# Recurrent scan of layer 2: subtractions and products of the queries' side moved from GpSimd to VectorE

## The reference, cut to what matters

```
def hgrn2_scan(q, k, v, logf, s0):
    ...
    def step(S, inp):
        qc, kc, vc, gc = inp
        bcs = jnp.cumsum(gc, axis=1)
        o_inter = jnp.einsum('bthk,bhkv->bthv', qc * jnp.exp(bcs), S)
        diff = bcs[:, :, None] - bcs[:, None]
        dec = jnp.exp(jnp.where(mask[None, :, :, None, None], diff, -jnp.inf))
        att = jnp.einsum('bthk,btshk,bshk->bhts', qc, dec, kc)
        o_intra = jnp.einsum('bhts,bshv->bthv', att, vc)
        last = bcs[:, -1]
        S_new = S * jnp.exp(last)[..., None] + jnp.einsum(
            'bshk,bshv->bhkv', kc * jnp.exp(last[:, None] - bcs), vc)
        return S_new, o_inter + o_intra
```

## Time and profile before

| what | value |
|---|---|
| median of three runs | 2851.33 us |
| the profiled execution | 2844.31 us |
| its span | 2842.5 us |
| TensorE busy over the span | 2559.0 us (90%) |
| VectorE busy | 1454.2 us (51%) |
| ScalarE busy | 753.1 us (26%) |
| GpSimd busy | 803.5 us (28%) |

### The profile page before, as it was taken

The page is one execution under the profiler, slowest core; times in us unless marked ns, Lnnn a source line. Parts: engine busy times, 40 slices in busy tenths (PEclk is TensorE's granted clock), DMA queues, the critical chain, the costliest instruction groups (busy, mean ns, idle before and its releaser), DMA issues.

```text
span 2842.5 us, 30129 instructions
## 1 busy us (share of the span) xinstructions
PE 2559.0 (90%) x11915; PEld 1877.4 (66%) x11915; DVE 1454.2 (51%) x1956; ACT 753.1 (26%) x1265; POOL 803.5 (28%) x429
## 2 busy tenths in 40 slices
PE   5789999998988879999988967789999799989997
PEld 3789854446877778644468957685445699864444
DVE  6866643335746677433456489773333426640013
ACT  1223221003554442200033344421010333130111
POOL 3547300003543432000026479710000347500000
PEclk6899899998999998999989988879999899979999
DMA  7734659990321146499915410155989133538880
GB/s 267 246 108 122 206 188 348 344 347 31 109 87 60 60 126 215 168 338 343 354 39 170 133 36 22 33 178 214 348 326 338 60 105 104 152 123 300 298 297 36
DMA packets 291851, 524.41 MB, mean 184 GB/s; under 512 B 9472, under 2 KB 141056, under 8 KB 291328
## 3 DMA queue, kind: packets, MB, share of 16 engines
q1 hardware_dynamic: 288256, 519.33, 51.9%
q10 hardware_dynamic: 3456, 3.15, 0.3%
HBM read 517.73 MB, written 4.72 MB: 184 GB/s over the span
## 4 chain that ended last, share of the span: by engine, by line
PE 70%; DVE 12%; ACT 4%; issue 3%; DMA 2%; POOL 2%; ACTq 0%; SPq 0%; DVEq 0%
PE ps L1924 23%; PE ps L1941 12%; PE ps L1661 6%; PE ps L1662 5%; PE ps L1663 5%; PE ps L1729 2%; DVE uw L1352 2%; PE ps L1862 1%; PE ps L1886 1%; DVE macc L2017 1%; PE ps L1887 1%; POOL wlo L1591 1%; PE ps L1763 1%; PE ps L1962 1%; PE ps L1963 1%
## 5 line engine op out<-in xcount | busy, mean ns | idle before, releaser
L1591 POOL TENSOR_TENSOR wlo<-ring,whi 128x1024 fp32r<-128x1024 f32 x202 | 535.2, 2666 | 1428.6 <-ACT whi L1458 1428.6
L1924 PE MATMUL ps<-ring,xg 128*128 128x512 f32 x1536 | 702.8, 595 | 0.0
L1924 PEld LDWEIGHTS ps<-ring,xg 128*128 128x128 f32 x1536 | 280.9, 191 | 296.3 <-issue 296.0
L2017 DVE SCALAR_TENSOR_TENSOR macc<-ring,cond_s,macc 128x1024 f32<-128x1024 f32 x280 | 387.1, 1441 | 4.8 <-DMA ring<-w_mod 4.8
L2241 DVE SCALAR_TENSOR_TENSOR hid<-ps,cws,sg 128x256 f32<-128x256 f32 x96 | 46.4, 484 | 652.6 <-ACT sg L1552 652.6
L1941 PE MATMUL ps<-ring,hidt 128*128 128x512 f32 x768 | 351.2, 601 | 2.3 <-ACT hidt L1527 2.3
L1661 PE MATMUL ps<-hh,whi 128*128 128x384 f32 x840 | 302.8, 360 | 33.3 <-POOL wlo L1591 20.6
L1662 PE MATMUL ps<-hl,whi 128*128 128x384 f32 x840 | 290.8, 346 | 0.0
L1663 PE MATMUL ps<-hh,wlo 128*128 128x384 f32 x840 | 290.4, 346 | 0.0
L1458 ACT ACTIVATE whi<-ring 128x1024 fp32r<-128x1024 f32 x202 | 207.0, 1054 | 278.2 <-DMA ring<-gmlp_w_out 82.7
L1941 PEld LDWEIGHTS ps<-ring,hidt 128*128 128x128 f32 x768 | 147.1, 193 | 183.4 <-issue 183.4
(11 more groups left out here) (366 smaller groups left out, 4193.4 us busy)
## 6 DMA issues: line engine op xcount, KB each, us to landing
ring<-moe_w_gu SPq DMA_DIRECT2D x192, 1024.0 KB, 8.0
ring<-w_mod SPq DMA_DIRECT2D x96, 1024.0 KB, 8.3
ring<-moe_w_down SPq DMA_DIRECT2D x96, 1024.0 KB, 6.2
ring<-gmlp_w_in SPq DMA_DIRECT2D x32, 1024.0 KB, 6.3
ring<-ssd_w_in SPq DMA_DIRECT2D x21, 1024.0 KB, 5.3
ring<-hgrn_w_in SPq DMA_DIRECT2D x20, 1024.0 KB, 5.2
ring<-gmlp_w_out SPq DMA_DIRECT2D x16, 1024.0 KB, 6.8
ring<-ssd_w_out SPq DMA_DIRECT2D x8, 1024.0 KB, 5.9
```

Of the source, the lines that this page charges most:

```text
L1591: pool.tensor_tensor(split_sub(wlo, s0), raw_sub(s0), split_sub(whi, s0).bitcast(F32), ALU.subtract).then_inc(S["lo_ready"], 1)
L1924: ins = pe.matmul(ps[:, s % 2, :], xg[:, w, k, :], whole(what, s, 4)[:, k % 4, :], start=(k == 0), stop=(k == KD - 1))
L2017: ins = dve.scalar_tensor_tensor(out=acc[:, v, :], in0=w[:, k, :], scalar=by, in1=acc[:, v, :], op0=ALU.mult, op1=ALU.add)
```

## The change

The subtraction and the product of the queries' side move from GpSimd's program into VectorE's, each right behind its counterpart of the keys' side. Their operands and their arithmetic stay the same, as do the semaphores that they raise (`w_sub`, `wq_ready`). GpSimd keeps `hqe` and the weight splits.

```diff
@@ pool_hgrn
-            def decay(n):
-
-                h, j = n // LEVELS, LEVELS - 1 - n % LEVELS
-                if n >= 3:
-                    pool.wait_ge(S["lv_done"], step_of(n - 3) + 1)
-                out = uw_slot(n)[:, 1, :].rearrange("p (b two x) -> p b two x", two=2, x=1 << j)
-                pool.tensor_tensor(out, crossed(h, j), border(h, j, True), ALU.subtract).then_inc(S["w_sub"], 1)
-
-            decay(0)
             for n in range(LEVELS * HH):
                 h, j = divmod(n, LEVELS)
-                if n + 1 < LEVELS * HH:
-                    decay(n + 1)
-                pool.wait_ge(S["u_exp"], n + 1)
-                W = uw_slot(n)[:, 1, :]
-                pool.tensor_tensor(W, W, hq[:, h, :], ALU.mult).then_inc(S["wq_ready"], 1)
                 if j == 5:
                     pool.wait_ge(S["qe_exp"], h + 1)
...
@@ dve_hgrn, produce(g)
                 dve.tensor_tensor(out, border(h, j), paired(hf_flat, h, j), ALU.subtract).then_inc(S["u_sub"], 1)
+                out = uw_slot(g)[:, 1, :].rearrange("p (b two x) -> p b two x", two=2, x=1 << j)
+                dve.tensor_tensor(out, crossed(h, j), border(h, j, True), ALU.subtract).then_inc(S["w_sub"], 1)
@@ dve_hgrn, complete(g)
                 dve.tensor_tensor(out, out, paired(hk_flat, h, j), ALU.mult).then_inc(S["uw_ready"], 1)
+                W = uw_slot(g)[:, 1, :]
+                dve.tensor_tensor(W, W, hq[:, h, :], ALU.mult).then_inc(S["wq_ready"], 1)
```

## The result

The changed kernel took 2853.52 us, the median of 20 runs (2847.01 to 2859.52), against 2850.4 us for 20 runs of the kernel before on the same chip (2845.11 to 2852.87). The ratio is 1.0016, with an interval of 1.0009 to 1.0023: the means lie 4.5 us apart, the medians 3.1. So it is slightly slower. That lies inside the forecast range and within the 0.2% that I had called "same", but on the other side of zero: I had forecast 3 us faster. That the range holds it is owed to its width and not to the sum, of which two terms were off.

A forecast was written before the change was run, and what follows sets the result against it. VectorE was taken to bound the scan's levels. Its work -4.0, waits +1.5 and -0.5 ahead of the stretch summed to -3.0 us, from 2851.3 to 2848.3 us, called "same"; range 2837 to 2861.

The forecast's parts named there:

- What bounds the kernel: In the scan's levels, VectorE sets the length: busy 167.2 of 177.6 us, idle 10.4.
- The mechanism of the hold: VectorE operations with two SBUF operands stand still until GpSimd's ends: 1.0 us per `hqe`, 2.1 per split, 20.6 in all.
- The work of VectorE: In the levels, 52.1 us new work plus 20.6 remaining holding less 76.7 holding before: -4.0 us.
- Sum 142.5 us: VectorE's own operations in the levels after the change, without holding, priced from start to start in quiet places.
- The waits: VectorE's idle time in the levels would go from 10.4 to 11.9 us: +1.5 us.
- The new wait at the head's start: VectorE waits for ScalarE's exponent of level 3, 0.7 us in each of seven heads: 4.9 us.
- 4.0 ... two waits at the ends of heads 3 and 5 ... I keep these: VectorE's waits for the diagonal's products, 1.19 and 2.78 us, would stay as they were.
- a rival with a chance of 0.21: TensorE falls to its lower clock behind splits; 2.78 us in all six heads gives +10 us, 2861; chance 0.21.
- "-0.5 us" ahead of the stretch: Before the levels, VectorE's second decayed key, 0.82 us under GpSimd's first two subtractions, gets shorter: -0.5 us.
- Edits at nothing: ScalarE's exponents, GpSimd's earlier split and the stages behind the scan were priced at no change.
- Too full: Rival: VectorE's operations keep their present lengths, so 52.1 us new work less 10.4 idle gives +42 us, 2893; chance 0.04.
- More is freed: Rival: remaining holding 7 us lower and half the 11.9 us of waits gone; halfway -9.5 us, 2842; chance 0.30.

The follow-up runs named there:

- e3: The changed kernel with the six weight splits that fall into the scan cut to two columns of one row: ratio 0.9963.
- e6: The changed kernel with the six weight splits and the eight `hqe` products moved from GpSimd to VectorE: 2831.86 us, ratio 0.9933.
- e11: The kernel before with the six splits and eight `hqe` products moved to VectorE, the queries' side left on GpSimd: ratio 0.9942.
- e12: The kernel before, unchanged, run and profiled once more: ratio 1.0002.
- e4: The changed kernel with the six weight splits done by VectorE between a head's last two masked copies: ratio 0.9951.
- e5: The kernel before with only the six weight splits moved from GpSimd to VectorE: ratio 0.9955.
- e1: The changed kernel with 21 unused TensorE products per head in heads 1 to 6, ahead of the held level product: ratio 1.0011.
- e10: The changed kernel with the 21 unused TensorE products per head, run again: ratio 1.0008.
- e2: The changed kernel with GpSimd's weight split put off until the exponent of the head's last level is there: ratio 1.0025.

## Why the prediction was wrong

**What bounds the kernel** held. VectorE is the path before and after: 167 us busy in either, and every run that shortened the stretch by more than 5 us took 6 us or more off its busy time (e3 to e6, e11).

**The mechanism of the hold** held, and its sizes too. I took 1.0 us for `hqe` and 2.1 for a split; head 5 shows 0.82 and 2.15. The whole of it can be told from e6, where nothing holds VectorE: 158.2 us less eight `hqe` at 0.60 and six splits at 1.13 from start to start leaves 146.6 us for the changed kernel's own operations. Of its 166.6 busy us, 20.0 is then holding, where I had 20.6. The Trainium skill's exclusive lock ("SBUF — State Buffer", section "Who interferes with whom") agrees: the held product ends 0.41 us behind the split, 1776.56 + 2.70 against 1776.15 + 2.70.

**The work of VectorE, "-4.0 us",** is the first step that failed. It came out at 166.6 - 167.2 = -0.6. With the holding right, the term at fault is "Sum 142.5 us" for the operations alone: it is 146.6, 4.1 more. I had priced every operation by the quiet level of a head's start. At the level with blocks of one token both subtractions and the keys' product take 0.64 to 0.67 us instead of 0.55 (L1331 at 1780.78 above, and in e6, without GpSimd, L1327 and L1329 at 1766.35), 0.57 from start to start instead of 0.465; three such operations in eight heads are 2.5 us. The other 200 subtractions and products stand 0.469 us apart in e6, which is 0.8 more; the last 0.8 is spread thinly. As the old holding had been taken as what remained of a fixed total, each microsecond missing in the price of an operation stood there as holding that would go.

**The waits, "+1.5 us",** are the second, with +4.3 (14.7 against 10.4).

- The new wait at the head's start came as described, for seven heads and for the exponent: 3.1 us, where I had 4.9.
- The last head: its product no longer stands behind `hqe`, but TensorE is not earlier for it. VectorE's waits there are 0.19 and 1.55 us for the levels, and 1.26 for the diagonal as before, where I had 1.0 for the levels.
- "4.0 ... two waits at the ends of heads 3 and 5 ... I keep these" is the largest miss among them. It became 8.5 us in six heads. (Of the two waits one did not recur: in e12 the kernel before has only head 5's, 2.76 us.) The mechanism stood in the text as a rival with a chance of 0.21, and its place (the split in the middle of the head, shorter steps behind it) was right. The price was not: 0.52 to 1.88 us in each head with a split, not 2.78, and the sign that I had named for it, 2 us and more, was not reached. Nor does such a wait need the long operation: e3, without it, still has 5.1 us in these heads. I had held against it that four heads with a split had no such wait before. Their order was another: there GpSimd's subtraction and product stood between `hqe` and the split, and now nothing does, so both holds fall into adjoining steps and TensorE idles 4.2 us at a stretch (2.5 at most before). That this order is why the wait spread is argued and not shown.

**"-0.5 us" ahead of the stretch:** the decayed key's mean fell from 718 to 339 ns, but the starts of the stretch scatter by 10 us between executions (1649.7 to 1660.2), so that its effect on the end can't be read.

**The sum** by the two traces is then -0.6 + 4.3 = +3.7 in the stretch, against +4.5 by the ratio of the times. Either miss alone would have left the forecast near zero (-0.6 + 1.5 - 0.5 = +0.4, and -4.0 + 4.3 - 0.5 = -0.2); it took both to make the kernel slower.

**Edits at nothing** held for ScalarE's exponents and behind the scan. For the split it did not: "comes earlier in the head, and TensorE needs it only in the next heads" is true of its result, and the time for which it holds VectorE I had priced. What I put at nothing is that TensorE stands idle while VectorE is held there. With the splits on VectorE in both kernels the change is worth -2.7 us of stretch (e4 against e5), though the times don't show it.

**Too full** (+42 us) did not happen: VectorE's busy time did not grow. **More is freed** did not either: the holding that stays is 20.0 us and not 7 less than the 20.6, and the waits grew.

Shown are the price of the operations (e6), the price of the splits in both kernels (e3, e4, e5), the part of TensorE's clock in the stretch (e1, e10), and that the exchange of 112 short operations is even, as far as the times can tell, once GpSimd makes no long ones (e6 and e11). Why the low clock spread to every head with a split stays open. The nearness of `hqe` and split is one guess, but e2, which parts them, has the low clock before the split begins, e3 without the split still reads 0.83, and e6 without either reads 0.83 to 0.92 where e11 has 1.00. So a part of it comes with the move itself. No run kept the clock at 1.00 in the changed kernel without giving TensorE more to do.

## What to carry to other kernels

When an operation on a neighbouring engine holds the bound engine, price it by the time for which it holds it, and compare that with what the bound engine would need to do it itself: here 2.15 against 1.13 us for the split and 0.82 against 0.60 for `hqe`, so in the stretch the help was worth less than nothing. Look for the few long operations first (six splits: 13 us of holding), since moving the many short ones (112 operations, 131 us of GpSimd's time) came out even. And a quantity that was found as what is left of a total carries every error of the terms that were taken off; measure the terms in the places that differ before you bank on the remainder.

## What the runs showed of the hardware

The Trainium skill ("Perfetto Trace Analysis", section "Optimizing Scalar/DVE Operations") has it that work may be taken off a saturated VectorE, and that between VectorE and GpSimd, which share a read port, this might not help. The runs here bear out the second and go beyond it: with GpSimd given nothing in these levels (e6), VectorE does 126 operations more than in the kernel before and is busy 158.2 instead of 167.2 us, and the kernel is 0.67% faster.

TensorE with 21 useless products more per head finished its heads 0.8 to 1.8 us earlier (e1, heads 2 to 6), and it came out of the hold at 2.4 GHz (0.91 us for six products) and not at 1.2 (1.62 us).

A subtraction or a keys' product of 128x384 on VectorE with blocks of one token took 0.65 us, with longer blocks 0.55, with GpSimd idle as well (e6).
